# Latent attention inside a fused two-block kernel: the query's RMS scale carried by the exponential, per-pair work dealt out again over the steps, a new head, and rope products on GpSimd

## The reference

```python
lat = h @ w_in                                   # 256 | 128 | 64 columns
q  = (rms_norm(c_q,  q_a_gain)  @ w_qb ).reshape(B, S, 8, 192)
kv = (rms_norm(c_kv, kv_a_gain) @ w_kvb).reshape(B, S, 8, 256)
k  = concat([kv[..., :128], broadcast(k_rope)], -1);  v = kv[..., 128:]
q, k = rms_norm(q, q_gain), rms_norm(k, k_gain)  # over 192 features, per head and token
q  = concat([q[..., :128], rope(q[..., 128:])], -1);  k likewise
p  = softmax(q @ k.T * 192 ** -0.5)
o  = p @ v;   return o.reshape(B, S, 1024) @ w_o
```

## Time and profile before

| | us |
|---|---|
| median of 3 runs | 2909.74 |
| lowest and highest of them | 2908.79, 2910.47 |
| the profiled execution's own time | 2907.81 |
| its span, first to last instruction | 2906.0 |
| latent attention's head in it | about 933 to 949 |
| its 32 steps | about 949 to 1074 |

### The profile page before, as it was taken

The page is one execution under the profiler, slowest core; times in us unless marked ns, Lnnn a source line. Parts: engine busy times, 40 slices in busy tenths (PEclk is TensorE's granted clock), DMA queues, the critical chain, the costliest instruction groups (busy, mean ns, idle before and its releaser), DMA issues.

```text
span 2906.0 us, 35630 instructions
## 1 busy us (share of the span) xinstructions
PE 2870.8 (99%) x13308; PEld 2375.8 (82%) x13308; DVE 1105.6 (38%) x2254; ACT 1622.0 (56%) x2410; POOL 407.3 (14%) x472
## 2 busy tenths in 40 slices
PE   9999999999999999999999999999999999999999
PEld 7989889888887678888887887888877788788887
DVE  6554736211214754211225114523244611642235
ACT  7675767544445765444556545545455644654555
POOL 1111111111111001111110111111111011111110
PEclk9999999999999999999999999999999999999999
DMA  8676867788887329988895797888878488778884
GB/s 248 152 159 138 178 135 159 167 191 194 194 191 165 88 46 202 195 193 194 192 196 117 153 194 165 198 194 195 183 182 188 91 182 193 168 187 191 202 194 116
DMA packets 137004, 499.11 MB, mean 172 GB/s; under 512 B 15344, under 2 KB 15600, under 8 KB 136720
## 3 DMA queue, kind: packets, MB, share of 16 engines
q0 software_dynamic: 67296, 245.59, 47.5%
q1 hardware_dynamic: 68688, 249.59, 28.6%
q10 hardware_dynamic: 864, 1.78, 0.2%
HBM read 494.81 MB, written 2.10 MB: 171 GB/s over the span
## 4 chain that ended last, share of the span: by engine, by line
PE 91%; DVE 3%; ACT 3%; DMA 1%; DVEq 1%; issue 1%; ACTq 0%
PE ps L1138 74%; PE ps L1157 5%; PE ps L1499 3%; PE ps L1257 1%; DMA wl<-weights 1%; PE ps L1646 1%; PE ps L1440 1%; PE ps L1419 1%; ACT arena L1009 1%; PE ps L1624 1%; PE ps L1218 0%; PE ps L1240 0%; DVE arena L2315 0%; DVE XT L2250 0%; PE ps L1215 0%
## 5 line engine op out<-in xcount | busy, mean ns | idle before, releaser
L470 ACT ACTIVATE wh<-raw 128x1024 fp32r<-128x1024 f32 (+1 forms) x465 | 489.9, 1053 | 932.3 <-PE ps L1138 900.0
L1138 PE MATMUL ps<-HH,wh 128*128 128x512 f32 x2224 | 870.4, 391 | 2.7 <-DVE HL L2258 2.1
L1138 PE MATMUL ps<-HH,wl 128*128 128x512 f32 x2224 | 865.8, 389 | 0.0
L1138 PE MATMUL ps<-HL,wh 128*128 128x512 f32 x2224 | 865.5, 389 | 0.0
L454 POOL DMA_DIRECT2D wl<-weights x465 | 405.4, 872 | 2463.4 <-ACT wl L474 2463.2
L1138 PEld LDWEIGHTS ps<-HH,wh 128*128 128x128 f32 x2224 | 417.6, 188 | 93.6 <-issue 4.4
L1138 PEld LDWEIGHTS ps<-HL,wh 128*128 128x128 f32 x2224 | 417.6, 188 | 87.3 <-issue 1.4
L1138 PEld LDWEIGHTS ps<-HH,wl 128*128 128x128 f32 x2224 | 417.5, 188 | 87.3
L474 ACT ACTIVATE wl<-raw 128x1024 fp32r<-128x1024 f32 (+1 forms) x465 | 483.7, 1040 | 0.0
L1138 PE MATMUL ps<-MH,wh 128*128 128x512 f32 x1056 | 411.9, 390 | 0.8 <-DVE ML L2138 0.7
L1138 PE MATMUL ps<-MH,wl 128*128 128x512 f32 x1056 | 410.9, 389 | 0.0
(11 more groups left out here) (334 smaller groups left out, 3017.3 us busy)
## 6 DMA issues: line engine op xcount, KB each, us to landing
raw<-weights SPq DMA_DIRECT2D x468, 512.0 KB, 5.4
wl<-weights POOLq DMA_DIRECT2D x465, 512.0 KB, 7.8
XT<-x SPq DMA_DIRECT2D x4, 512.0 KB, 8.3
out<-XT SPq DMA_DIRECT2D x3, 512.0 KB, 2.7
arena<-tables POOLq DMA_DIRECT2D x1, 1024.0 KB, 11.1
arena<-table_h ACTq DMA_DIRECT2D x1, 640.0 KB, 5.7
arena<-swaps_a POOLq DMA_DIRECT2D x1, 576.0 KB, 8.0
out<-XT SPq DMA_DIRECT2D x2, 256.0 KB, 2.4
```

What stands on the lines that cost most here:

```text
L470: act_f(wh[:, n, 0:w], raw[:, n, 0:w], ACT.Copy)
L1138: op = mm(bank(g, t), w[:, slot, at:at + P], x[:, first + kt, :], start=(kt == 0 and w is wh and x is xh), stop=(kt == n_k - 1 and w is wl ...
```

## The change

- The query tiles are no longer multiplied by `rs_q`. ScalarE puts the gains in as it copies out of PSUM (`m_gained`). The query's squares are summed with tokens on the partitions: eight matmuls whose stationary side is a 128 x 128 block of squares and whose moving side is 16 columns of ones (`m_query_sums`), instead of two of 512 columns. The scale is then one number per partition for each block of queries, `q_scale(j)`: Ln and Exp over 128 x 8 numbers (`m_query_scale`). It becomes the scale of the exponential (`m_exp`) and a factor in the negation of the maximum.
- The rope tile is not multiplied by `rs_q` either; `rope_high` and `rope_low` split it. For pairs 1 to 3, GpSimd does the five products of the rotation (`query_rope`): it stands in its queue behind the DMA of slab 5, 7 and 9 of the stretch, waits for `mp_gained` and `mp_taken`, and tells VectorE by `mp_rotated`.
- Lags: the second projected tile is the rope tile; VectorE adds at lag 5 and splits at 5 to 7; the values move from lag 5 to 6 on TensorE and from 6 to 7 on ScalarE, with the slab's high part behind them.
- The head projects the rope tile first, then the keys, then the other query tiles; it sums the keys' squares only; the values follow; the query's squares are summed ahead of step 1, behind step 0's projection. The swap matmul and `m_idle` are gone.

The diff, cut:

```diff
+            rope_slabs = tuple(LATENT_SLAB + k for k in (5, 7, 9))
+            def query_rope(pair):
+                x = m_in[pair % 2][:, 2, :]
+                pool.wait_ge(mp_gained, pair + 1)
+                pool.wait_ge(mp_taken, pair)
+                nc.gpsimd.tensor_tensor(t1, x, tab[:, 2, :], ALU.mult)
+                for b in (0, 64):
+                    pool.drain()
+                    nc.gpsimd.tensor_tensor(t2[b:b + 32, :], x[b + 32:b + 64, :], tab[b + 32:b + 64, 3, :], ALU.mult)
+                    pool.drain()
+                    nc.gpsimd.tensor_tensor(t2[b + 32:b + 64, :], x[b:b + 32, :], tab[b:b + 32, 3, :], ALU.mult)
+                pool.drain().then_inc(mp_rotated, 1)
...
+            def m_query_scale(b, pair):
+                dst = q_scales(pair)
+                act.wait_ge(mp_sum, 2 * pair + 1 if pair else 2)
+                op = act_f(dst, ps[:, b, 0:P:16], ACT.Ln, scale=1.0 / 192, bias=cst[:, C_EPS6:C_EPS6 + 1])
...
-            m_exp = exp_row(S, smM, lambda j: smM[j % 3], B_SCALE)
+            def m_exp(j, at):
+                act.wait_ge(att_m, at.value(1))
+                act_f(smM[j % 3], smM[j % 3], ACT.Exp, scale=q_scale(j), bias=col[:, 2 + j % 2:3 + j % 2],
+                      accum_out=col[:, 4 + j % 2:5 + j % 2]).then_inc(att_e, 1)
...
+            def m_query_sums(n, b):
+                pe.wait_ge(mp_added, n)
+                for k in range(M_PER):
+                    h, r = k // 4, slice(k % 4 * P, (k % 4 + 1) * P)
+                    op = mm(ps[:, b, 16 * k:16 * k + 16], m_sq[:, h, r], ones[:, 0:16], start=True, stop=True)
+                op.then_inc(mp_sum, 1)
...
+                if j == 1:
+                    m_query_sums(2, 2)
+                    pe.wait_ge(mp_rs, 1)
...
+                if j == 0:
+                    dve.wait_ge(mp_rs, 2)
+                dve.drain()
+                v.tensor_scalar(col[:, 2 + j % 2:3 + j % 2], col[:, j % 2:j % 2 + 1], q_scale(j), -1.0, ALU.mult, ALU.mult)\
```

More of the change, by code:

```diff
@@ L784, in m_copies, with m_gained, m_key_scale @@
                 return act_f(m_in[pair % 2][:, first:first + n, :], ps[:, b:b + n, :], ACT.Copy)
+            def m_gained(b, n, first, pair, gain):
+                return act_f(m_in[pair % 2][:, first:first + n, :], ps[:, b:b + n, :], ACT.Identity,
+                             scale=par[:, gain:gain + 1])
             def m_values(b, pair):
                 return act_f(vM2[pair % 2][:, :, :], ps[:, b:b + 2, :].rearrange("p b (t s) -> p (b t) s", s=256), ACT.Copy)
-            def m_scale(b, dst, n):
-                act.wait_ge(mp_sum, n + 2)
-                act_f(dst, ps[:, b:b + 2, :], ACT.Ln, scale=1.0 / 192, bias=cst[:, C_EPS6:C_EPS6 + 1]).then_inc(mp_free, 1)
+            def m_key_scale(b, pair):
+                dst = rs_k[pair % 2]
+                act.wait_ge(mp_sum, 2 * pair + 2 if pair else 1)
+                op = act_f(dst, ps[:, b:b + 2, :], ACT.Ln, scale=1.0 / 192, bias=cst[:, C_EPS6:C_EPS6 + 1])
+                if pair:
+                    op.then_inc(mp_free, 1)
@@ L1393, in _ @@
             m_weights(0)
-            for t in range(3):
-                op = m_q(0, t, t)
-            op.then_inc(w_used, 1)
+            m_q(0, 2, 3).then_inc(mp_rope, 1)
             m_weights(1)
@@ L1451, in m_project @@
                     m_q(pair, 0, 5)
-                    m_q(pair, 1, 6).then_inc(mp_proj, 1)
+                    m_q(pair, 2, 6).then_inc(mp_proj, 1)
                 pair = m_at(j, 1)
@@ L2019, in _, with rope_start, rope_rest, rope_whole @@
                 v.tensor_tensor(kr_lo[r, h, :], kR[r, :], kr_hi[r, :], ALU.subtract)
[L2021 to L2027 removed]
+            def rope_start(pair):
+                x = m_in[pair % 2][:, 2, :]
+                dve.wait_ge(mp_gained, pair + 1)
+                v.tensor_tensor(t1, x, tab[:, 2, :], ALU.mult)
+                swap32(t2, x, 0)
+            def rope_rest(pair):
+                swap32(t2, m_in[pair % 2][:, 2, :], 64)
+            def rope_whole():
+                dve.drain()
+                v.tensor_tensor(xg, t1, t2, ALU.add)
+            def rope_high(pair, h):
+                r = slice(64 * h, 64 * h + 64)
+                op = v.tensor_tensor(qr2[pair % 2][r, h, :], t1[r, :], t2[r, :], ALU.add)
+                if h:
+                    op.then_inc(mp_taken, 1)
+            def rope_low(pair, h):
+                r, other = slice(64 * h, 64 * h + 64), slice(64 - 64 * h, P - 64 * h)
                 dve.drain()
[L2029 removed]
+                v.tensor_tensor(qr2[pair % 2][other, h, :], xg[r, :], qr2[pair % 2][r, h, :], ALU.subtract)\
+                    .then_inc(mp_done, 1)
             a = c.take("att", M_STEPS)
```

173 lines of the change are left out of this document (63 added, 110 removed).

## The result

The changed kernel took 2914.78 us (median of 14 runs, 2912.6 to 2919.14) against 2909.28 of before on the same chip (14 runs, 2907.37 to 2910.55). The ratio is 1.0020 with a 95% interval of 1.0013 to 1.0028, so it is slower by 5.5 us: clearly slower, though its median is within the 0.2% (5.8 us) that the prediction called no change. The forecast was a gain of 1.0. The profiled execution's span is 2911.9 us, against 2906.0.

What follows compares the result with a forecast made beforehand. TensorE, busy 99% of the span at full clock, was taken as the bound, with time only in its waits or moved matmuls. Head +4.4, stalls -5.4, other parts nil: -1.0 from 2909.74 gives 2908.7 us, range 2905.5 to 2915.5.

Steps and rivals of the forecast that it cites:

- Part 1: VectorE in the steps: 6.6 us less work per pair, so TensorE's four waits for its division go, 5.4 us gained.
- Part 2: TensorE's query sums: two of 512 columns (1.75 us) become sixteen MATMULs of 16 columns (1.70 us), nothing gained or lost.
- Part 3: ScalarE in the steps: query scale falls from 2.2 to 0.2 us, exponential at most 0.1 a step more, all hidden.
- Part 4: GpSimd's fifteen rotation products: 7 us a pair within 16.8 us before they are needed, so the cost is nil.
- The rival: GpSimd's products in lags 1 to 3 exclude VectorE's adds and divisions: 2911.5 to 2922 us; chance 0.12.
- slack of 2.6 us: Steps: time between VectorE's chain and TensorE's need for it, taken to absorb lateness caused by GpSimd.
- Part 5: The head: in the new order TensorE gets the banks for lag 1 later, 4.4 us lost by lag 2.
- The rival of the clock: Head: two new TensorE gaps of 4.9 us drop the clock; one fall 2911.5 us, two 2914.2; chance 0.30.

Runs made afterwards that it cites:

- fill: The changed kernel with four matmuls of constants ahead of the keys' sums and four more behind step 1's scores; median 2908.65 us.
- head: The changed kernel with only the head reordered on VectorE, TensorE and ScalarE, plus two idle matmuls ahead of the keys' sums; median 2909.32 us.
- early: The changed kernel with GpSimd's rotation products ahead of a slab's transfer instead of behind it (slabs 4, 6, 8); median 2913.50 us.
- slabs: The changed kernel with ScalarE's parts of two slabs ahead of the query's scale in the head; median 2911.52 us.
- head2: The run head with five idle matmul calls added between the values and score 0, GpSimd's products kept; median 2906.53 us.
- twice: The run fill with each of GpSimd's 15 products issued twice; median 2912.57 us.
- best: The changed kernel with the order of head and the rotation of pairs 1 to 3 on VectorE, none on GpSimd; median 2904.00 us.
- best3: The run best with two idle matmul calls between the values and score 0; median 2900.84 us, ratio 0.9983 to before.

## Why the prediction was wrong

**Part 1 (VectorE in the steps, -5.4): right.** All four waits of the earlier trace rows are gone in after, and the offset falls by 1.3, 1.8, 1.8 and 0.6 at steps 8, 16, 24 and 25. VectorE did less by 14.2 us in the steps, where part 1 gives 19.8 for three pairs; the missing 5.6 are GpSimd's doing (adds of 3.45, 3.24 and 2.26 us for 1.38 make 4.8, a division of 1.07 for 0.49 another 0.6).

**Part 2 (sums, nil): right.** Sixteen 16-column matmuls at 954.55, the next matmul at 956.25: 1.70.

**Part 3 (ScalarE): right.** 0.27 and 0.21 for 128 x 8, with 0.2 taken; the exponential 0.80 to 0.82 for 0.71, with at most 0.1 allowed.

**Part 4 (GpSimd, nil): wrong, and one of two terms that decided it.** The size was right, 1.27 a product with 1.4 taken, and no wait of VectorE for the rotation appeared. The 1.27 also agrees with the 1.1 to 1.3 that the prediction estimated from the Trainium skill (GPSIMD Engine Reference, section 3), whose figure is for an add, not a product. The step that failed is the question asked: what does GpSimd's work delay by being late? It should have been what it delays by running. The rival had the mechanism, at a chance of 0.12, and argued it away with a slack of 2.6 us. That slack is the one between a row's chain and its transposes. The adds stand under another deadline: TensorE wants its sums in the next step. In pair 2 the division and the adds were late by 2.4 us (0.58 and 1.86) and TensorE waited 1.24, so the slack was 1.2. And the part assumed that the products start when their input is ready; the second of five started 1.3 to 9 us after the first's end, behind the slab's transfer, and in pairs 1 and 2 that is among the adds. Cost in after: +3.2, of which a stall of about 1.3 (fill's, at the full clock) and the rest the clock.

**Part 5 (the head, +4.4): right.** At the full clock fill gives 4.2 at step 2 and 4.4 at step 3. The head's loss was ScalarE's slab parts behind a late sum and VectorE's order, and both could be mended (head, 0.3 at step 2).

**The rival of the clock: underrated, its price too high.** It was given 0.30, on gaps of 4.9 us of a length that the trace of before did not hold. Both gaps came (4.66, 4.58) and the clock fell behind both. The Trainium skill (TensorE: Matmul & The Clock Gate, Part 1) says that an idle array goes back to 1.2 GHz, and behind these two gaps (4.66 and 4.58 us) the trace agrees. The only rule that bore on a gap longer than any in the trace spoke for the rival, and no row against it. I had both facts and still made "no fall" the forecast. The term measured 1.75 and 1.6 where 2.5 and 3.0 were the upper prices, because the slow stretches were shorter than the 8.24 us from which the price was taken. Behind the first gap matmuls are slow from 944.69 to about 949, behind the second from 963.03 to about 966, where the first two were not slow. The price itself also had a weak source: in the row of the kernel's first matmuls the profile shows the granted clock at 1.00, so no row shows that those twelve were slow because of the clock.

With both put right the sum reads +4.4 + 1.75 + 1.6 + 3.2 - 5.4 = +5.55. The range to 2915.5 held the result; the point did not, as two rivals that it treated as alternatives came together, with one setting off the other's mechanism a third time.

## What to carry over

A gap that a change opens on TensorE has a price beyond its length; find every one of a few microseconds in the new order, and either close it or lay matmuls of constants in it, counted as the trace counts them. When an idle engine takes work over, ask beside which instructions it will run, not only by when it must be done, and what in its own queue stands ahead. And a summed balance of order, stalls and clock should be tested by taking each away alone: here the same edits, with the head put in another order and the rotation left on VectorE, turned +5.5 us into -5.0.

## What of the hardware was not expected

- **A GpSimd product behind a slab transfer waits for it.** The first product runs at once, the second only about 8 us after the row of the transfer (8.5 and 8.2 in after, 7.8 and 7.7 in head, 8.3 and 8.2 in fill; 9.8 once, in early). Behind the second of two transfers together it was 9.8 to 11.3. With none just ahead the pause was 0.32. That GpSimd is still writing the transfer's descriptors is my reading of it; no row names the work, the profile calls it issue.
- **The clock can fall without a long gap, and among short gaps the length does not tell.** Ahead of the sixteen 16-column matmuls of the query's sums it fell behind waits of 1.24 us (after), 1.45 and 0.65 (slabs), 1.53 (early), 0.83 (head) and 0.91 (head2), and it held behind waits of 1.16 (head2), 1.05 (fill), 0.81 (twice) and 0.64 (head) ahead of the same sums. Ahead of score 0 a wait of 2.25 us let it fall in best and not in head, with the same matmuls on both sides. Ahead of pair 1's projection it held behind 2.54 (slabs). What tells these apart the runs don't show; no run has sums of another shape. What is shown is that filling the wait in best3 removed the spread (2.3 us instead of 6).
- **Exclusion costs both sides.** Two adds went from 1.38 to 3.2 to 3.45 us beside products that themselves went from 1.27 to 1.54, and a division with one input in SBUF from 0.49 to 1.07.
